# Other start addresses for the two parts of the activations

## What is computed

```python
u = rms_norm(h, norm_mix_pre[l])
(q_n, kc_n, vc_n, ks_n, vs_n, kw_n, vw_n, g_n,
 q_s, k_s, v_s, gate_a, gate_b) = jnp.split(u @ w_in[l], IN_OFFSETS, axis=-1)
...
y = jax.nn.sigmoid(gate_a) * (o_a @ w_up_nsa[l]) + jax.nn.sigmoid(gate_b) * (o_b @ w_up_swa[l])
h = h + rms_norm(y @ w_out[l], norm_mix_post[l])
u = rms_norm(h, norm_mlp_pre[l])
f = jnp.square(jax.nn.relu(u @ w_mlp_in[l])) @ w_mlp_out[l]
h = h + rms_norm(f, norm_mlp_post[l])
...
def swiglu(h, w_in, w_out):
    gu = h @ w_in
    g, u = jnp.split(gu, 2, axis=-1)
    return (jax.nn.silu(g) * u) @ w_out
```

## Time and profile before

| | |
|---|---|
| median of 3 runs | 1342.05 us (1341.38 to 1342.37) |
| profiled execution | 1342.27 us, its span 1340.2 us |
| TensorE busy (matmuls) | 1309.1 us, 98% of the span |
| TensorE busy (weight loads) | 1083.9 us, 81% |
| VectorE busy | 926.9 us, 69% |
| ScalarE busy | 661.7 us, 49% |
| mean granted clock of TensorE | 0.997 of 2.4 GHz |

### The profile page before, as it was taken

One profiled execution on the slowest core, in us unless ns is written; L12 is line 12 of the kernel. 1 busy time (PEld: TensorE's weight loads), 2 busy tenths in 40 slices (PEclk: granted clock), 3 DMA queues, 4 the chain that ended last, 5 costly groups with the idle time before them and its releaser, 6 DMA issues.

```text
span 1340.2 us, 16397 instructions
## 1 busy us (share of the span) xinstructions
PE 1309.1 (98%) x6611; PEld 1083.9 (81%) x6611; DVE 926.9 (69%) x1023; ACT 661.7 (49%) x928; POOL 28.3 (2%) x56
## 2 busy tenths in 40 slices
PE   8998999999999999999999999999999999999998
PEld 8986677888887888888788888788888887788887
DVE  5368888776658776677876667966766786744444
ACT  5355765645456344445534445753444566644442
POOL 2200010000000000000000000000000000000000
PEclk9999999999999999999999999999999999999999
DMA  8997668777775787884678785588787632455551
GB/s 251 253 352 210 189 228 320 283 292 270 281 284 204 258 275 281 281 281 162 240 259 283 281 309 166 180 303 277 255 282 281 222 126 96 157 188 188 189 189 63
DMA packets 162762, 317.98 MB, mean 237 GB/s; under 512 B 7128, under 2 KB 108944, under 8 KB 153472
## 3 DMA queue, kind: packets, MB, share of 16 engines
q1 hardware_dynamic: 158800, 305.44, 66.4%
q0 software_dynamic: 3712, 11.45, 3.3%
q10 hardware_dynamic: 176, 0.05, 0.0%
HBM read 314.56 MB, written 1.84 MB: 236 GB/s over the span
## 4 chain that ended last, share of the span: by engine, by line
PE 88%; DVE 7%; ACT 3%; issue 1%; DMA 1%; SPq 0%; DVEq 0%; ACTq 0%
PE bank L735 27%; PE bank L737 27%; PE bank L736 27%; PE bank L833 2%; DVE full L1951 2%; DVE wlo L1855 1%; PE bank L756 1%; PE bank L759 1%; DMA raw<-in_cmp_w_v 1%; DVE xt L1939 1%; DVE mix L1937 1%; PE bank L783 1%; ACT whi L1376 1%; PE bank L1091 1%; DVE mix L1951 0%
## 5 line engine op out<-in xcount | busy, mean ns | idle before, releaser
L1855 DVE TENSOR_TENSOR wlo<-raw,whi 128x2048 fp32r<-128x2048 f32 x202 | 462.5, 2291 | 223.4 <-ACT whi L1376 223.3
L1376 ACT ACTIVATE whi<-raw 128x2048 fp32r<-128x2048 f32 x205 | 392.2, 1914 | 181.8 <-PE bank L737 167.4
L735 PE MATMUL bank<-whi,uhi 128*128 128x512 f32 (+2 forms) x1168 | 454.1, 389 | 7.8 <-DVE ulo L1964 5.1
L737 PE MATMUL bank<-whi,ulo 128*128 128x512 f32 (+2 forms) x1168 | 445.2, 381 | 0.0
L736 PE MATMUL bank<-wlo,uhi 128*128 128x512 f32 (+2 forms) x1168 | 444.3, 380 | 0.0
L735 PEld LDWEIGHTS bank<-whi,uhi 128*128 128x128 f32 x1168 | 219.9, 188 | 53.6 <-issue 12.9
L737 PEld LDWEIGHTS bank<-whi,ulo 128*128 128x128 f32 x1168 | 219.6, 188 | 43.2
L736 PEld LDWEIGHTS bank<-wlo,uhi 128*128 128x128 f32 x1168 | 220.1, 188 | 40.0 <-issue 0.5
L735 PE MATMUL bank<-whi,hsplit 128*128 128x512 f32 (+1 forms) x512 | 198.0, 387 | 0.0
L737 PE MATMUL bank<-whi,hsplit 128*128 128x512 f32 (+1 forms) x512 | 195.9, 383 | 0.0
L736 PE MATMUL bank<-wlo,hsplit 128*128 128x512 f32 (+1 forms) x512 | 195.8, 382 | 0.0
(11 more groups left out here) (263 smaller groups left out, 952.8 us busy)
## 6 DMA issues: line engine op xcount, KB each, us to landing
raw<-in_ffn_w_in SPq DMA_DIRECT2D x176, 512.0 KB, 4.7
ada<-in_ada_w SPq DMA_DIRECT2D x72, 1024.0 KB, 7.2
raw<-in_ffn_w_out SPq DMA_DIRECT2D x44, 1024.0 KB, 5.0
raw<-in_w_in SPq DMA_DIRECT2D x16, 1024.0 KB, 8.5
raw<-in_w_mlp_in SPq DMA_DIRECT2D x16, 1024.0 KB, 6.7
raw<-in_w_mlp_out SPq DMA_DIRECT2D x16, 1024.0 KB, 4.9
ada<-in_kv_ada_w SPq DMA_DIRECT2D x8, 1024.0 KB, 7.1
raw<-in_w_kv SPq DMA_DIRECT2D x8, 1024.0 KB, 5.0
```

The source lines that it names most:

```text
L735: nc.tensor.matmul(o, sh, mh, start=start, stop=False, skip_group_check=skip)
L737: return nc.tensor.matmul(o, sl, mh, start=False, stop=stop, skip_group_check=skip)
L1376: ins = nc.scalar.activation(whi[:, ring(n), :], raw[:, ring(n), :], ACT.Copy)
L1855: ins = nc.vector.tensor_tensor(wlo[:, ring(n), :], raw[:, ring(n), :], whi[:, ring(n), :].bitcast(F32), ALU.subtract)
```

## The change

Four tensors get another place in the order of the calls. `uhi`, `ulo`, `cst` and `gate3` move behind `adab`, in the order `ulo`, `gate3`, `uhi`, `cst`.

```diff
         full = sb("full", [P, KT, T])
-        uhi = sb("uhi", [P, KT, T], F32R)
-        ulo = sb("ulo", [P, KT, T], F32R)
         wide = sb("wide", [P, 4096])
         arena = sb("arena", [P, 5504])
         mix = sb("mix", [P, 2048])
         hsplit = sb("hsplit", [P, 2048], F32R)
         turned1 = sb("turned1", [P, 384])
-        cst = sb("cst", [P, NCST])
         vec = sb("vec", [P, 112])
         adab = sb("adab", [P, NMOD * KT])
+        ulo = sb("ulo", [P, KT, T], F32R)
+        gate3 = sb("gate3", [P, 2, 24])
+        uhi = sb("uhi", [P, KT, T], F32R)
+        cst = sb("cst", [P, NCST])
         mods = sb("mods", [P, NMOD, KT])
...
         sinks = sb("sinks", [P, 8])
-        gate3 = sb("gate3", [P, 2, 24])
         wg = sb("wg", [P, KT, 24])
```

## The result

The changed kernel takes 1352.86 us in the median of 6 runs (1351.22 to 1354.42) against 1342.07 us (1341.20 to 1346.41). The ratio is 1.0076, with a 95% interval of 1.0066 to 1.0086. The profiled execution has a span of 1351.4 us, 11.2 us more than before.

The account below looks back on a forecast made before the run. TensorE's matmuls were taken to bound the kernel, by count times distance. With 9.2 us less for matmuls on u and 0 for all else, 1342.1 - 9.2 = 1332.9, said as 1333 us; range 1316 to 1363.

Parts of the forecast that it names:

- What bounds the kernel: TensorE's matmul lines 735 to 737: time is the count of matmuls times the distance between their starts.
- The term for the matmuls with u as weights: 3672 matmuls on `uhi` and `ulo`, loaded or streamed: distance 2.5 ns shorter each, 9.2 us less in all.
- the compression stage: Stage with weights at ever other offsets: 117.5 against 120.0 ns for 256 columns, taken as 2.5 ns less per matmul.
- The upper bound: Matmuls on u would at worst keep the unsettled 232 ns seen after transposes, 5.3 ns more each, 19.5 us more.
- the beat does not settle: Rival, chance 0.33: with changing load offsets all 3672 matmuls on u stay near 232 ns, 19.5 us more, 1361.5 us.
- The range: Whole kernel, 1316 to 1363 us: from half of the 13.3 ns gone to slightly beyond the whole unsettled distance.
- slower: Whole kernel takes longer than before, chance 0.33, against faster 0.46 and same 0.21.
- No effect: Rival, chance 0.21: load and stream reads do not meet, the 13.3 ns are hand-over between matmuls; 1342 us.
- `hsplit` at cost 0: 3 x 480 matmuls with `hsplit` as weights keep weights and stream at 0: distance stays 226.7 ns, cost 0.
- `cst` at 0: Transposes using the identity in `cst`, moved to 256 modulo 512: paced by the weight load, so cost 0.
- The writes of `uhi` and `ulo` at 0: VectorE and ScalarE instructions writing both parts, 631 and 687 ns: no dependence on 64 bytes seen, cost 0.
- The matmuls with 128 columns: 144 matmuls at 112 ns, paced by the weight load alone: set apart as under half a microsecond.

Follow-up runs that it names:

- e_lo64: Against the kernel before, only `ulo` begins at 64 bytes modulo 512, `uhi` stays at 0: 1351.90 us, ratio 1.0061.
- a_cst256: Against the kernel before, only `cst` moves to 256 bytes modulo 512; `uhi` and `ulo` lie elsewhere but still at 0: 1342.99 us, ratio 1.0004.
- 192: Against the kernel before, `uhi` and `ulo` both begin at 192 bytes modulo 512: 1345.79 us, ratio 1.0022.

## Why the prediction was wrong, point by point

- **What bounds the kernel** was right. The mean distance of the matmuls on u, times their number, gives 9.8 us of the 11.2 between the spans, and the instructions of VectorE and ScalarE took what they took.
- **The term for the matmuls with u as weights** is the step that failed. "I take 2.5 ns less all the same", 9.2 us less, should have been 3.2 ns more for the matmuls with 512 columns, 88% of the 3672, and 0.3 to 1.8 ns less for those with 256: 9.5 us more in all. The sign came from the compression stage, the row that the text itself called imperfect. It was imperfect twice. Its weights have half the columns; and it has 256 columns of stream, where offsets do gain, as the table shows, while with 512 columns all seven places off the period lost. I carried a gain from the 256-column form over to the 512-column form. Whether the doubt raised there was right (half the load may cost half of 13.3 ns), no run shows; it isn't needed, since 256 columns with all 128 columns of weights read 117.7 ns with u loaded, on the mean of the seven places off the period, as that stage does with 117.5.
- **The upper bound** of 232 ns from the transients was near the price of an offset common to both parts, 229.2 to 234.0 ns measured, but no bound: six of the seven places lie over it. The rival "the beat does not settle" came nearest to the mechanism and put it at 1361.5 us. What it did not see is that 256 is no offset at all, so that only a third of the loads (`ulo`) was out of place, and that the row settles after all, into a pattern of three lines. `e_lo64` shows both, with 1351.9 us. A third out of place is no fixed price either: with `ulo` it is 230.9 ns on the mean, with `wlo` in one line of three 231.9.
- **The range** of 1316 to 1363 held the time, and "slower" had 0.33 of the chance. The point, 1333, was on the wrong side. A range of 47 us that reaches to both sides of 1342 says little of the change, so that it held is no support for the forecast.
- **"No effect"** and the Trainium skill's rule in "TensorE: Matmul & The Clock Gate", Part 2 (two independent read ports, so that a weight load takes no read bandwidth from the running matmul): the runs do not agree with the absence of any effect. Moving only `hsplit`, the loaded operand, by 64 bytes takes the distance in settled blocks from 226.7 to 233.4 ns; moving both operands by 64 bytes changes nothing. In these runs the load and the running matmul do bear on each other.
- **`hsplit` at cost 0** was nearly right: 0.4 us spill over from neighbouring blocks, which I had not counted. **`cst` at 0** was right, by `a_cst256`. **The writes of `uhi` and `ulo` at 0** were right: 631 and 687 ns in both profiles. **The matmuls with 128 columns**, set apart, were right to be: 110.5 to 110.6 ns on the mean in every kernel, wherever u began.

What is shown: the distance of these matmuls depends on where the loaded operand begins against the streamed one, and 256 bytes apart is as good as 0; equal places give a settled 226.7 ns (32 cycles of 2.4 GHz over the 512 columns), and with 512 columns none of the other seven multiples of 32 is as good. Places between multiples of 32 bytes were not tried. What is argued only: that the two readers meet in some part of SBUF that comes round every 256 bytes, and that with equal places they fall into a fixed order. What stays open: why 192 costs a fifth of its neighbours, why 256 columns gain where 512 lose, why the long distance of the pattern stands after line 737, and what chooses between the two speeds at 64. No kernel of these beats the one before.

## What to carry to other kernels

When matmuls with float32r operands and 512 columns run back to back and each loads new weights, keep the stationary and the moving operand at the same place modulo 256 bytes in SBUF. With 256 columns equal places were not the fastest, and with 128 they made no difference. Here one tensor out of place cost 0.6% (`ulo`), 0.7% (`hsplit`) or 1.25% (`wlo`), both parts of u together 0.2 to 1.5%, and a small tensor ahead of a large one is enough to do it. To see it, look at the distances between starts in a long undisturbed block: with 512 columns here one constant number meant equal places, and a sequence of two to fifteen numbers in turn meant that the operands stood apart. And a price read from another shape is not a price: even its sign may be that shape's own.

## What the runs showed of the hardware that I had not expected

- 256 bytes are a full period (0.9999, 0.9990 to 1.0009) and 128 are not (1.0110).
- The cost is no matter of degree: 32 bytes cost 233.2 ns, as much as 64 (233.4) and 160 (233.4).
- Out of place is not disorder: each kernel repeats its own sequence of distances, one matmul long at equal places, three in the changed kernel (228, 229, 236 ns), fifteen with `wlo` at 64.
- The same form at the same places can run at two speeds, 117.6 and 113.5 ns with both parts at 64 and 256 columns.
- The same offset slows one shape and speeds up another: at 192, 512 columns 229.2 instead of 227.6 ns, and 256 columns 113.6 instead of 119.9.
- With `ulo` at 64 the long distance is recorded after line 737, not where its load runs. Blocks on `hsplit` at 0 inherit the state of the block before: 227.3 instead of 227.05 ns in the changed kernel, about 228.2 with u at 96 and 160.
